# The last 16 keys of the scores in one padded block, and half of head 0's v transfers from ScalarE

## The chip, the cores and the metric

The kernel runs on one core of a Trainium2 chip. The metric is the device time of one execution, in microseconds (us).

## The reference

A two-layer encoder works on 272 tokens (16 learned meta tokens and 256 of the sequence) of width 1024. The change touches its first sub-layer alone, retention with four heads:

```python
q = rotary(q.astype(jnp.float32).reshape(B, T, RET_HEADS, RET_QK_DIM), pos)
k = rotary(k.astype(jnp.float32).reshape(B, T, RET_HEADS, RET_QK_DIM), pos) * (RET_QK_DIM ** -0.5)
...
s = jnp.einsum("bhid,bhjd->bhij", qc, kc) * intra_decay
o = jnp.einsum("bhij,bhje->bhie", s, vc) + jnp.einsum("bhid,bhde->bhie", qc, R) * q_decay
```

Taken in both directions this is, for each head, scores of all pairs of the 272 tokens, multiplied by gamma to the power of the tokens' distance, and then the product with v (512 columns for each head). Group norm, a gate and an output projection follow; then a gated convolutional MLP, a gated linear recurrence and a second MLP.

## The kernel before

All matrices are multiplied in two float16 parts. A float32 operand is split into a high part (its float16) and a low part (what is left), and each product is made of three: high with high, high with low, low with high (`three`, L1656 to L1660). The weights come from memory in chunks of 2 MB, each in two halves, into two `stage` buffers; ScalarE makes the high part (L548, the call `prep`) and VectorE the low part (L1008, also `prep`), in quarters. Four quarters make a chunk, and TensorE waits for each. TensorE's order is written out by hand, and so is every other engine's: each engine's program is one list in which an instruction that waits holds all that stand behind it.

For each head h the chunks are 3h (v's weights), 3h + 1 (q and k) and 3h + 2 (the gate). TensorE's order in a head is: values (chunk 3h, made at the end of the head before), q and k, gate, scores (L1908 to L1914), the values of the next head, for which it first waits on `g_out`, and the output products (L1922 to L1933). Behind them it waits for `v_out` of the next head before it takes chunk 3h + 4 (L1896).

- VectorE turns v out of PSUM by 32 x 32 blocks (`v_evict`, L1169 and L1170, raising `v_out`), rotates q and k (L1268 to L1271), makes their low parts (`qk_low`, L1241), evicts the gate (L1162, raising `g_out`), multiplies the scores by the decay (L1295), makes v's means (L1280) and low parts (L1285), and the low parts of the scores (L1303, L1304).
- ScalarE makes q's and k's high parts (`qk_high`, L700), scales v's rows (L719), makes v's high part (L726, L727) and that of the scores (L734 to L738), and does the gate's nonlinearity (L740).
- SyncE moves v from the 32 x 32 blocks into rows, in 16 transfers of 32 KB and 4 smaller ones for the last 16 tokens (`load_v_rows`, L472 to L482), each of which raises `v_landed`. In between it issues the chunk loads (L456).

The 272 tokens are cut into tiles of 128, 128 and 16 keys. The scores of a tile are a matmul with the keys as the stationary operand, for two halves k of the head's 256 features:

```python
for n, (m0, m) in enumerate(TOK_TILES):
    key = slice(m0, m0 + m)
    mm = three(ps[0:m, A + n, 0:T], qk_hi[:, 2 + k, key], qk_lo[:, 2 + k, key],
               qk_hi[:, k, :], qk_lo[:, k, :], k == 0, k == 1)
```

The output product of the last 16 keys is a single one already. Its 80 rows hold high scores at row 0, their low part at row 32 (`R_HI`) and the high scores again at row 64 (`R_LO`), against v's high, high and low parts (L1931).

Of the kernel before, what the change touches and what calls it, by code (L numbers as in the profile page):

```python
# [33 lines left out]
F16 = mybir.dt.float16  # L34
# [4 lines left out]
P = 128  # L39
# [109 lines left out]
def build(nc, tokens, gains, lru_pars, ffn_pars, chunks, ident, rope, decay, out):  # L149
    ctx = ExitStack()  # L150
    with ctx:
# [54 lines left out]
        rotq = carve(4, T)  # L206
        v_blocks = carve(4, 2 * P)
        v_edge = carve(4, 32)
        v_rows = carve(8, P)
# [19 lines left out]

        R_HI, R_LO = 32, 64  # L230

# [213 lines left out]
        def _(sp):  # L445
# [26 lines left out]
            def load_v_rows(h):  # L472

                sp.wait_ge(v_out, h + 1)
                from_blocks = v_blocks.rearrange("p e (n m) -> p (e n) m", m=P)
                for f in range(4):
                    for r in range(4):
                        rows, cols = slice(32 * r, 32 * (r + 1)), slice(32 * f, 32 * (f + 1))
                        sp.dma_start(v_rows[rows, :, cols], from_blocks[cols, :, rows]).then_inc(v_landed, 16)
# [47 lines left out]
        def _(act):  # L527
# [167 lines left out]
            for h in range(HEADS):  # L695
                c = RET_IN[h]

                def qk_high(x):
                    act.wait_ge(rot_done, 2 * h + x + 1)
                    act.activation(halves(qk_hi, x), halves(rotq, x), ACTF.Copy).then_inc(qkhi_made, 1)  # L700

                for q in range(3):
                    prep(c + 2, q)
                if h:
                    head_squares(h - 1)
                prep(c + 2, 3)
                for q in range(SUB if h else 1):
                    prep(c + 3, q)
# [12 lines left out]
                for n, (_, m) in enumerate(TOK_TILES):  # L721
                    act.wait_ge(vmean, NTT * h + n + 1)
                    if (h, n) == (0, 2):
                        act.wait_ge(zeroed, 1)
                    if n == 2:
                        act.activation(v_hi4[R_HI:R_HI + m, n], vs[n][0:m], ACTF.Identity, bias=vsum[0:m, n, 1:2])  # L726
                    act.activation(v_hi4[0:m, n], vs[n][0:m], ACTF.Identity,  # L727
# [7 lines left out]
                if h == 0:  # L735
                    act.wait_ge(zeroed, 2)
                act.activation(s_hi[R_LO:R_LO + META, 2, :], sT[0:META, 2, :], ACTF.Copy)
# [246 lines left out]
        def _(dve):  # L984
# [250 lines left out]
            for h in range(HEADS):  # L1235
# [3 lines left out]
                def qk_low(x):  # L1239
                    dve.wait_ge(qkhi_made, 2 * h + x + 1)  # L1240
                    dve.tensor_tensor(halves(qk_lo, x), halves(rotq, x), halves(qk_hi, x),  # L1241
                                      ALU.subtract).then_inc(qklo_made, 1)
# [51 lines left out]
                for n, (m0, m) in enumerate(TOK_TILES):  # L1294
                    last = dve.tensor_tensor(sT[0:m, n, :], ps[0:m, A + n, 0:T],  # L1295
                                             decay_sb[0:m, h, 2 * P - m0:2 * P - m0 + T], ALU.mult)
                last.then_inc(s_dec, 1)
                if h:
                    rsqrt(rs, A + 3, 0, ESTIMATE[("head", h - 1)])
                else:  # L1300
                    v_halves()
# [311 lines left out]
        def _(pool):  # L1613
# [25 lines left out]
            for n, size in enumerate((D, HEAD_V)):  # L1639
                pool.memset(ones_sb[:, n, :], 1.0 / size).then_inc(ones_set, 1)  # L1640
            pool.memset(v_hi[:, 2, :], 0.0).then_inc(zeroed, 1)
            pool.memset(s_hi[:, 2, :], 0.0).then_inc(zeroed, 1)
# [12 lines left out]
        def _(pe):  # L1655
# [236 lines left out]
            for h in range(HEADS):  # L1892
# [15 lines left out]
                for k in range(2):  # L1908
                    pe.wait_ge(qklo_made, 2 * h + k + 1)
                    for n, (m0, m) in enumerate(TOK_TILES):  # L1910
                        key = slice(m0, m0 + m)
                        mm = three(ps[0:m, A + n, 0:T], qk_hi[:, 2 + k, key], qk_lo[:, 2 + k, key],
                                   qk_hi[:, k, :], qk_lo[:, k, :], k == 0, k == 1)
                mm.then_inc(s_up, 1)  # L1914
# [9 lines left out]
                for e in range(4):  # L1924
# [3 lines left out]
                    for n in range(2):  # L1928
                        three(ps[:, A + e, 0:T], v_hi[:, n, col], v_lo[:, n, col], s_hi[:, n, :], s_lo[:, n, :],
                              n == 0, False)  # L1930
                    mm = pe.matmul(ps[:, A + e, 0:T], v_hi[0:R_LO + META, 2, col], s_hi[0:R_LO + META, 2, :],  # L1931
                                   start=False, stop=True)
# [280 lines left out]
```

## Time and profile before

| | |
|---|---|
| median of 3 runs | 708.3 us (708.06 to 708.33) |
| profiled execution | 708.33 us, span 706.5 us |
| TensorE busy | 695.9 us, 98% |
| VectorE busy | 610.5 us, 86% |
| ScalarE busy | 518.0 us, 73% |
| DMA | 134.31 MB, mean 190 GB/s |

The span runs from the first to the last recorded instruction; the time of the execution has 1.8 us more around it. Busy time of TensorE (PE) is modelled: a matmul of 272 columns is shown as 0.28 us long while the next one starts 0.12 us after it, so the starts are to be read, not the lengths. "Idle before" is the time in which an engine stood still ahead of a row, with what ended it.

### The profile page before, as it was taken

To read this page: it belongs to the slowest core of one execution; us is meant where nothing else is said; L and a number is where in the kernel's file an instruction comes from. 1 tells how busy PE (TensorE), PEld (TensorE's weight loads), DVE (VectorE), ACT (ScalarE), POOL (GpSimd) and SP (SyncE) were. 2 spreads that over 40 slices of the span, in tenths; PEclk is the share of its full clock that TensorE was granted. 3 is DMA by queue.
4 is the path that set the end of the run, shared out by engine and by line. 5 is a ranking of instruction groups with operands and counts; after the bars stand their busy time and mean duration, and the time that the engine had idled before them with its cause. 6 is when DMAs were issued, how large, how long until landed. Compare 5 with 4: busy or idle time off the path is not lost.

```text
span 706.5 us, 15923 instructions
## 1 busy us (share of the span) xinstructions
PE 695.9 (98%) x6495; PEld 584.7 (83%) x6495; DVE 610.5 (86%) x828; ACT 518.0 (73%) x834; POOL 25.7 (4%) x26
## 2 busy tenths in 40 slices
PE   8999999999999999999999999999999999999996
PEld 6888787887899888888889998888788888885464
DVE  6979897978789799989898879999999999999543
ACT  7477766757566888878787777999769888987431
POOL 0002020110100000000003000000000000000000
PEclk9999999999999999999999999999999999999999
DMA  9965646453481355655589951110625565566821
GB/s 348 309 250 149 240 140 250 131 175 147 180 321 48 133 217 188 229 178 178 187 307 397 350 192 61 62 60 1 234 92 211 195 223 208 208 237 207 260 41 60
DMA packets 47323, 134.31 MB, mean 190 GB/s; under 512 B 29728, under 2 KB 30240, under 8 KB 32032
## 3 DMA queue, kind: packets, MB, share of 16 engines
q1 hardware_dynamic: 46976, 133.20, 53.6%
q8 instruction: 39, 0.64, 0.4%
q10 hardware_dynamic: 288, 0.31, 0.1%
q14 instruction: 20, 0.16, 0.1%
HBM read 129.17 MB, written 1.05 MB: 184 GB/s over the span
## 4 chain that ended last, share of the span: by engine, by line
PE 89%; ACT 4%; DVE 4%; issue 1%; DMA 1%; SPq 0%; DVEq 0%; ACTq 0%
PE ps L1658 23%; PE ps L1660 22%; PE ps L1659 22%; PE ps L2094 3%; PE ps L2096 3%; PE ps L2095 3%; PE ps L1700 2%; PE ps L1705 2%; PE ps L1701 2%; PE ps L1782 1%; PE ps L1778 1%; PE ps L1779 1%; PE ps L2034 1%; DMA stage<-in_chunks 1%; ACT work L846 1%
## 5 line engine op out<-in xcount | busy, mean ns | idle before, releaser
L1658 PE MATMUL ps<-a_hi,w_hi 128*128 128x272 f16 (+1 forms) x1000 | 276.9, 277 | 0.3 <-DVE work L1170 0.3
L1660 PE MATMUL ps<-a_hi,w_lo 128*128 128x272 f16 (+1 forms) x1000 | 276.9, 277 | 0.0
L1659 PE MATMUL ps<-a_lo,w_hi 128*128 128x272 f16 (+1 forms) x1000 | 276.9, 277 | 0.0
L1008 DVE SCALAR_TENSOR_TENSOR w_lo<-stage,w_hi 128x1024 f16<-128x1024 f32 x207 | 247.8, 1227 | 26.4 <-ACT w_hi L548 26.1
L548 ACT ACTIVATE w_hi<-stage 128x1024 f16<-128x1024 f32 x207 | 210.1, 1047 | 50.6 <-PE ps L1660 21.6
L1658 PEld LDWEIGHTS ps<-a_hi,w_hi 128*128 128x128 f16 x1000 | 97.8, 98 | 17.1 <-issue 0.7
L1660 PEld LDWEIGHTS ps<-a_hi,w_lo 128*128 128x128 f16 x1000 | 97.8, 98 | 15.9
L1659 PEld LDWEIGHTS ps<-a_lo,w_hi 128*128 128x128 f16 x1000 | 97.9, 98 | 15.9
L1658 PE MATMUL ps<-y_hi,w_hi 128*128 128x272 f16 (+3 forms) x496 | 106.1, 242 | 0.0
L1659 PE MATMUL ps<-y_lo,w_hi 128*128 128x272 f16 (+3 forms) x496 | 106.1, 242 | 0.0
L1660 PE MATMUL ps<-y_hi,w_lo 128*128 128x272 f16 (+3 forms) x496 | 106.0, 242 | 0.0
L778 ACT ACTIVATE work<-work,cpar 128x272 f32<-128x272 f32 (+1 forms) x96 | 50.5, 596 | 40.4 <-DVE work L1162 40.4
L1658 PEld LDWEIGHTS ps<-y_hi,w_hi 128*128 128x128 f16 x496 | 48.5, 98 | 3.4 <-issue 0.2
L1659 PEld LDWEIGHTS ps<-y_lo,w_hi 128*128 128x128 f16 x496 | 48.5, 98 | 3.3
L1660 PEld LDWEIGHTS ps<-y_hi,w_lo 128*128 128x128 f16 x496 | 48.5, 98 | 3.0
L1359 DVE SCALAR_TENSOR_TENSOR work<-work,cpar 128x271 f32<-128x271 f32 (+1 forms) x96 | 40.9, 489 | 2.2 <-ACT work L778 2.2
L782 ACT ACTIVATE work<-work,cpar 128x271 f32<-128x271 f32 (+1 forms) x96 | 41.2, 500 | 0.0
L2096 PE MATMUL ps<-w_hi,y_lo 128*128 128x512 f16 (+1 forms) x120 | 40.4, 336 | 0.0
L2094 PE MATMUL ps<-w_hi,y_hi 128*128 128x512 f16 (+1 forms) x120 | 40.4, 336 | 0.0
L2095 PE MATMUL ps<-w_lo,y_hi 128*128 128x512 f16 (+1 forms) x120 | 40.4, 336 | 0.0
L1162 DVE TENSOR_TENSOR work<-ps,rs_in 128x1032 f32<-128x1032 f32 (+1 forms) x26 | 32.7, 1256 | 8.3 <-PE ps L1660 8.2
L1658 PE MATMUL ps<-work 128*128 128x272 f16 (+2 forms) x120 | 33.4, 278 | 0.5 <-ACT y_hi L836 0.5
(281 smaller groups left out, 1084.3 us busy)
## 6 DMA issues: line engine op xcount, KB each, us to landing
stage<-in_chunks SPq DMA_DIRECT2D x118, 1024.0 KB
work<-work SPq DMA_DIRECT2D x96, 32.0 KB, 2.0
stage<-in_chunks SPq DMA_DIRECT2D x3, 512.0 KB
decay_all<-in_decay SPq DMA_DIRECT2D x1, 1056.0 KB, 13.4
out<-sq SPq DMA_DIRECT2D x4, 256.0 KB, 2.0
hT<-in_tokens SPq DMA_DIRECT2D x3, 272.0 KB, 6.4
stage<-in_chunks SPq DMA_DIRECT2D x2, 256.0 KB
mT<-in_gains SPq DMA_DIRECT2D x1, 512.0 KB, 6.0
```

Of the source, the lines that this page charges most:

```text
L548: act.activation(part(0, c, q), flat(stage, c, q), ACTF.Copy, scale=W_SCALE).then_inc(whi_made, 1)
L778: last = act.activation(u_cv[b][:, n, t0:T], u_in[b][:, n, t0:T], ACTF.Identity, scale=tap_col(layer, j, 1, n), bias=tap_col(layer, j, 3, n))
L782: last = act.activation(u_left[:, n, t0:T - 1], u_in[b][:, n, t0:T - 1], ACTF.Copy, scale=tap_col(layer, j, 0, n))
L1008: dve.scalar_tensor_tensor(out=part(1, c, q), in0=flat(stage, c, q), scalar=W_SCALE, in1=part(0, c, q), op0=ALU.mult, op1=ALU.subtract).th ...
L1162: return dve.tensor_tensor(dst[:, :, t0:T], ps[:, first:first + 4, t0:T], rs_in[:, t0:T].unsqueeze(1).to_broadcast([P, 4, T - t0]), ALU.mult)
L1359: last = dve.scalar_tensor_tensor(out=u_cv[b][:, n, t0:T - 1], in0=u_in[b][:, n, t0 + 1:T], scalar=tap_col(layer, j, 2, n), in1=u_cv[b][:, ...
L1658: pe.matmul(o, w_h, x_h, start=start, stop=False)
L1659: pe.matmul(o, w_h, x_l, start=False, stop=False)
L1660: return pe.matmul(o, w_l, x_h, start=False, stop=stop)
L2094: pe.matmul(o, yh, wh[:, cols], start=k == 0, stop=False)
L2095: pe.matmul(o, yh, wl[:, cols], start=False, stop=False)
L2096: mm = pe.matmul(o, yl, wh[:, cols], start=False, stop=k == FT - 1)
```

## The change

It has two parts.

*Scores.* The stationary operand of the last 16 keys is no longer taken from `qk_hi` and `qk_lo`. A new tile `key_edge` of 2 x 128 columns, cleared once by GpSimd, gets the 16 keys' high part in columns 0 to 15 (ScalarE, in `qk_high`) and their low part in columns 32 to 47 (VectorE, in `qk_low`). Two products for each half k, with q's high and q's low part, take the place of three. Their rows 0 to 15 are then high keys by q, and rows 32 to 47 low keys by q. VectorE multiplies the second group by the decay on its own, right behind the rest, into row 96 (`R_KEY`) of the last scores tile, ScalarE copies v's high part to row 96 once more, and the output product takes 112 rows in place of 80.

*Transfers.* Of head 0's 16 transfers of v blocks, SyncE issues the first 8 and ScalarE the other 8, behind its fourth piece of the gate's weights. The other heads keep all 16 on SyncE.

```diff
+        key_edge = carve(P).bitcast(F16).rearrange("p (k c) -> p k c", k=2)
...
-                for f in range(4):
+                for f in range(4 if h else 2):
                     for r in range(4):
...
                     act.wait_ge(rot_done, 2 * h + x + 1)
+                    if (h, x) == (0, 0):
+                        act.wait_ge(zeroed, 1)
+                    act.activation(key_edge[:, x, 0:META], rotq[:, 2 + x, 2 * P:T], ACTF.Copy)
                     act.activation(halves(qk_hi, x), halves(rotq, x), ACTF.Copy).then_inc(qkhi_made, 1)
...
                 prep(c + 2, 3)
+                if h == 0:
+                    act.wait_ge(v_out, 1)
+                    for f in (2, 3):
+                        for r in range(4):
+                            rows, cols = slice(32 * r, 32 * (r + 1)), slice(32 * f, 32 * (f + 1))
+                            act.dma_start(v_rows[rows, :, cols], from_blocks[cols, :, rows]).then_inc(v_landed, 16)
...
                     if n == 2:
-                        act.activation(v_hi4[R_HI:R_HI + m, n], vs[n][0:m], ACTF.Identity, bias=vsum[0:m, n, 1:2])
+                        for row in (R_HI, R_KEY):
+                            act.activation(v_hi4[row:row + m, n], vs[n][0:m], ACTF.Identity, bias=vsum[0:m, n, 1:2])
...
                     dve.wait_ge(qkhi_made, 2 * h + x + 1)
+                    dve.tensor_tensor(key_edge[:, x, R_HI:R_HI + META], rotq[:, 2 + x, 2 * P:T], key_edge[:, x, 0:META],
+                                      ALU.subtract)
...
                 last.then_inc(s_dec, 1)
+                if h == 0:
+                    dve.wait_ge(zeroed, 3)
+                dve.tensor_tensor(s_hi[R_KEY:R_KEY + META, 2, :], ps[R_HI:R_HI + META, A + 2, 0:T],
+                                  decay_sb[R_HI:R_HI + META, h, R_HI:R_HI + T], ALU.mult)
...
+            pool.memset(key_edge[:], 0.0).then_inc(zeroed, 1)
...
-                    for n, (m0, m) in enumerate(TOK_TILES):
+                    for n, (m0, m) in enumerate(TOK_TILES[0:2]):
                         key = slice(m0, m0 + m)
-                        mm = three(ps[0:m, A + n, 0:T], qk_hi[:, 2 + k, key], qk_lo[:, 2 + k, key],
-                                   qk_hi[:, k, :], qk_lo[:, k, :], k == 0, k == 1)
+                        three(ps[0:m, A + n, 0:T], qk_hi[:, 2 + k, key], qk_lo[:, 2 + k, key],
+                              qk_hi[:, k, :], qk_lo[:, k, :], k == 0, k == 1)
+                    pe.matmul(ps[:, A + 2, 0:T], key_edge[:, k, :], qk_hi[:, k, :],
+                              start=k == 0, stop=False)
+                    mm = pe.matmul(ps[:, A + 2, 0:T], key_edge[:, k, :], qk_lo[:, k, :],
+                                   start=False, stop=k == 1)
...
-                    mm = pe.matmul(ps[:, A + e, 0:T], v_hi[0:R_LO + META, 2, col], s_hi[0:R_LO + META, 2, :],
+                    mm = pe.matmul(ps[:, A + e, 0:T], v_hi[0:R_KEY + META, 2, col], s_hi[0:R_KEY + META, 2, :],
                                    start=False, stop=True)
```

What each engine does where the change moves it, first ScalarE in head 0, from the last two pieces of the gate's weights (chunk 2) to those of head 1's values (chunk 3), before the change (a name behind "waits" is a semaphore):

```order
L548 ACTIVATE w_hi<-stage 128x1024 [waits w_used,w_landed0_1] x2
L548 ACTIVATE w_hi<-stage 128x1024 [waits w_used,w_landed1_0]
L700 ACTIVATE work<-work 128x2x272 [waits rot_done] x2
```

And the same place after it:

```order
L549 ACTIVATE w_hi<-stage 128x1024 [waits w_used,w_landed0_1] x2
L716 DMA work<-work 32x8x32 [waits v_out]
L716 DMA work<-work 32x8x32 x7
L549 ACTIVATE w_hi<-stage 128x1024 [waits w_used,w_landed1_0]
L703 ACTIVATE work<-work 128x16 [waits zeroed,rot_done]
L704 ACTIVATE work<-work 128x2x272
L703 ACTIVATE work<-work 128x16 [waits rot_done]
L704 ACTIVATE work<-work 128x2x272
```

Eight DMA issues stand ahead of the first piece of chunk 3, and a small copy ahead of each large one. Second, VectorE in head 0, from the low parts of q and k to v's means, before:

```order
L1241 TENSOR_TENSOR work<-work 128x2x272 [waits qkhi_made] x2
L1008 SCALAR_TENSOR_TENSOR w_lo<-stage,w_hi 128x1024 [waits w_used,whi_made] x3
L1162 TENSOR_TENSOR mT<-ps,rs_in 128x1088 [waits w_used]
L1295 TENSOR_TENSOR work<-ps,decay_all 128x272 [waits s_up]
L1295 TENSOR_TENSOR work<-ps,decay_all 128x272
L1295 TENSOR_TENSOR work<-ps,decay_all 16x272
L1280 TENSOR_SCALAR vsum<-vsum 128x1 [waits vs_out] x2
```

And after:

```order
L1252 TENSOR_TENSOR work<-work 128x16 [waits qkhi_made]
L1254 TENSOR_TENSOR work<-work 128x2x272
L1252 TENSOR_TENSOR work<-work 128x16 [waits qkhi_made]
L1254 TENSOR_TENSOR work<-work 128x2x272
L1019 SCALAR_TENSOR_TENSOR w_lo<-stage,w_hi 128x1024 [waits w_used,whi_made] x3
L1173 TENSOR_TENSOR mT<-ps,rs_in 128x1088 [waits w_used]
L1308 TENSOR_TENSOR work<-ps,decay_all 128x272 [waits s_up]
L1308 TENSOR_TENSOR work<-ps,decay_all 128x272
L1308 TENSOR_TENSOR work<-ps,decay_all 16x272
L1313 TENSOR_TENSOR work<-ps,decay_all 16x272 [waits zeroed]
L1293 TENSOR_SCALAR vsum<-vsum 128x1 [waits vs_out] x2
```

Two small subtractions stand among the low parts, and one more product with the decay ahead of the means.

## Rows read from the trace of the kernel before

**Rows 1.** The page's busy times, and the list of waits (us, times, longest).
```profile
PE 695.9 (98%) x6495; PEld 584.7 (83%) x6495; DVE 610.5 (86%) x828; ACT 518.0 (73%) x834; POOL 25.7 (4%) x26
...
PE ps L1658 <- DVE work L1170: 0.3, 1, 0.3
```

**Rows 2.** Timeline of TensorE, head 0 (start, us, what, idle before and its releaser).
```profile
43.79 0.29 PE L1658 MATMUL ps<-a_hi,w_hi 128*128 128x272 f16 x1
...
58.06 0.28 PE L1931 MATMUL ps<-work 80*128 80x272 f16 x1
58.61 0.29 PE L1658 MATMUL ps<-a_hi,w_hi 128*128 128x272 f16 x1 [0.27 <-DVE work L1170]
```

**Rows 3.** Timeline of ScalarE, head 0.
```profile
26.56 2.00 ACT L548 ACTIVATE w_hi<-stage 128x1024 f16<-128x1024 f32 x2 [0.49 <-DMA stage<-in_chunks]
29.05 1.06 ACT L548 ACTIVATE w_hi<-stage 128x1024 f16<-128x1024 f32 x1 [0.48 <-DMA stage<-in_chunks]
...
41.80 0.72 ACT L719 ACTIVATE work<-work,rs_tok 128x512 f32<-128x512 f32 x1 [1.80 <-DMA work<-work]
...
45.11 1.33 ACT L727 ACTIVATE work<-work,vsum 128x512 f16<-128x512 f32 x2 [1.09 <-DVE vsum L1280]
46.47 0.72 ACT L726 ACTIVATE work<-work,vsum 16x512 f16<-16x512 f32 x1
...
52.63 2.94 ACT L548 ACTIVATE w_hi<-stage 128x1024 f16<-128x1024 f32 x3
55.47 0.20 ACT L751 ACTIVATE lam<-par 128x16 f32<-128x16 f32 x1
```

**Rows 4.** Timeline of VectorE, head 0.
```profile
27.82 4.61 DVE L1008 SCALAR_TENSOR_TENSOR w_lo<-stage,w_hi 128x1024 f16<-128x1024 f32 x4
...
41.55 1.28 DVE L1162 TENSOR_TENSOR mT<-ps,rs_in 128x1088 f32<-128x1088 f32 x1
43.90 1.12 DVE L1295 TENSOR_TENSOR work<-ps,decay_all 128x272 f32<-128x272 f32 x3 [1.06 <-PE ps L1660]
...
53.70 3.50 DVE L1008 SCALAR_TENSOR_TENSOR w_lo<-stage,w_hi 128x1024 f16<-128x1024 f32 x3 [0.19 <-ACT w_hi L548]
...
58.28 0.27 DVE L1170 STREAM_TRANSPOSE work<-ps 128x128 f32<-128x128 f32 x1
```

**Rows 5.** Timeline of TensorE, scores of head 1.
```profile
81.32 0.28 PE L1658 MATMUL ps<-work 128*128 128x272 f16 x1
...
81.67 0.28 PE L1658 MATMUL ps<-work 128*128 128x272 f16 x1
...
81.90 0.28 PE L1660 MATMUL ps<-work 128*128 128x272 f16 x1
82.11 0.28 PE L1658 MATMUL ps<-work 128*16 128x272 f16 x1
...
83.59 0.28 PE L1660 MATMUL ps<-work 128*16 128x272 f16 x1
83.80 0.29 PE L1658 MATMUL ps<-a_hi,w_hi 128*128 128x272 f16 x1
```

**Rows 6.** DMA issues: SyncE's of v's rows (ns, then timeline), ScalarE's only two.
```profile
L479 SPq DMA_DIRECT2D work<-work x64: 591/611/1806, 25.5 to 146.8; - x64
...
25.46 11.79 SPq L479 DMA_DIRECT2D work<-work  x16
...
L673 ACTq DMA_DIRECT2D hT<-in_tokens x2: 404/428/452, 0.7 to 1.2; - x2
```

**Rows 7.** ScalarE's sequencer at L547 between 28 and 29 us.
```profile
L547 ACTq EVENT_SEMAPHORE  x1: 17/17/17, 28.3 to 28.3; - x1
```

**Rows 8.** Timeline of VectorE, heads 1 and 2.
```profile
81.41 1.29 DVE L1162 TENSOR_TENSOR mT<-ps,rs_in 128x1088 f32<-128x1088 f32 x1
...
120.64 1.29 DVE L1162 TENSOR_TENSOR mT<-ps,rs_in 128x1088 f32<-128x1088 f32 x1 [0.69 <-PE ps L1660]
123.48 1.12 DVE L1295 TENSOR_TENSOR work<-ps,decay_all 128x272 f32<-128x272 f32 x3 [1.55 <-PE ps L1660]
```

More of the change, by code:

```diff
@@ L207, in build @@
         v_blocks = carve(4, 2 * P)
+        from_blocks = v_blocks.rearrange("p e (n m) -> p (e n) m", m=P)
         v_edge = carve(4, 32)
@@ L228, in halves @@
             return v.rearrange("p (g x) t -> p x g t", x=2)[:, x]
-        R_HI, R_LO = 32, 64
+        R_HI, R_LO, R_KEY = 32, 64, 96
+        key_edge = carve(P).bitcast(F16).rearrange("p (k c) -> p k c", k=2)
         off = 0
@@ L474, in load_v_rows @@
                 sp.wait_ge(v_out, h + 1)
-                from_blocks = v_blocks.rearrange("p e (n m) -> p (e n) m", m=P)
-                for f in range(4):
+                for f in range(4 if h else 2):
                     for r in range(4):
@@ L723, in _ @@
                     if (h, n) == (0, 2):
-                        act.wait_ge(zeroed, 1)
+                        act.wait_ge(zeroed, 2)
                     if n == 2:
-                        act.activation(v_hi4[R_HI:R_HI + m, n], vs[n][0:m], ACTF.Identity, bias=vsum[0:m, n, 1:2])
+                        for row in (R_HI, R_KEY):
+                            act.activation(v_hi4[row:row + m, n], vs[n][0:m], ACTF.Identity, bias=vsum[0:m, n, 1:2])
                     act.activation(v_hi4[0:m, n], vs[n][0:m], ACTF.Identity,
@@ L735, in _ @@
                 if h == 0:
-                    act.wait_ge(zeroed, 2)
+                    act.wait_ge(zeroed, 3)
                 act.activation(s_hi[R_LO:R_LO + META, 2, :], sT[0:META, 2, :], ACTF.Copy)
```

## The prediction

> **What bounds the kernel now.** I began with the busy times and the list of waits: TensorE is busy for 98% of the span, and in the four heads it waits for another engine's result once after the start, 0.3 us for VectorE's transpose at L1170 [rows 1]. So a change in the heads is worth what it takes from TensorE's row of matmuls, less every new wait. The second view is TensorE's timeline around the scores; the third is ScalarE's and VectorE's timelines in head 0, where the reader is to see that both are busy almost without a gap from 43.9 us until VectorE hands head 1 its banks.
>
> The one wait is larger than 0.3 us: the last output product of head 0 starts at 58.06, the next matmul could start at 58.18 and starts at 58.61, so 0.43 us are lost; the transpose at 58.28 ends at 58.55 [rows 2, 4]. The chain behind it begins with the end of the scores, for which VectorE's multiplication by the decay waits until 43.90; the mean behind that lets ScalarE start the halves of v at 45.11 after 1.09 us of idle; ScalarE runs on to the weight piece that begins at 52.63 and ends at 53.7, and VectorE needs three pieces and the transpose from there [rows 3, 4]. In head 0 TensorE and this chain end 0.43 us apart, and the chain is the longer.
>
> **TensorE.** Two products in a row start 0.115 us apart. Head 1's scores run from 81.32 to 83.80, 2.48 us for 18 products, where 18 x 0.116 make 2.09. The missing 0.39 lies in four places: 81.90 to 82.11 before a block of 16 columns, 83.59 to 83.80 behind one, and the same twice more [rows 5]. No such gap stands between the two full blocks: the second starts at 81.67, three products behind 81.32. With the last block 128 columns wide and two products for its three, 16 x 0.116 = 1.86 us are left: **0.63 us less per head**, 0.23 from two products and about 0.39 from four gaps. The output product has 112 rows for 80 and the same 128 columns. I cost it at nothing; gaps like those above on both sides of each of its four would be 0.8 us per head, and nothing in the rows asks for them.
>
> **Small operations.** Per head ScalarE gets two copies of 128x16 and one more copy of v's last rows (16x512); VectorE gets two subtractions of 128x16 and one decay product of 16x272. A 128x16 operation takes 0.20 us on ScalarE [rows 3], and I take at most that on VectorE; the copy of v is 0.72 us [rows 3]; the decay product adds 1.12/3 = 0.36 us [rows 4]. GpSimd's extra clearing lies in the first microseconds, hidden behind the first loads.
>
> **The eight transfers on ScalarE.** An issue of this shape takes SyncE 0.61 us, and 16 of them 11.79 us with one of 1.8 us among them, or 0.66 us from start to start otherwise [rows 6]. ScalarE's only issues in the trace, of plain rows, take 0.43 us; SyncE's of v are nearest in shape, so I take 0.66; 0.45 and twice 0.66 are the ends that the rivals price. When do they begin? The two activations at 26.56 wait for a stage that lands at 26.5. ScalarE's sequencer passed the next wait at 28.3, when the second of them still ran until 28.56 [rows 3, 7]: it runs ahead of its engine. So the issues begin at about 26.7 and end at 26.7 + 8 x 0.66 = 32.0. Behind them stands the first piece of chunk 3 (29.05 now): it ends at about 33.1. VectorE wants its result as the fourth of the pieces that begin at 27.82, at 31.27 [rows 4]. **VectorE loses 1.8 us**, and from there to 42.83 it has no more than 0.2 us of idle to give back. What the move buys is no term: v's rows now land at 41.8 [rows 3], after a wait of 1.8 us, and still ScalarE's next step stands idle for 1.09 us, for the mean behind the scores. SyncE's loads go out 5 us earlier, for stages that nobody waits for there.
>
> **Head 0.** VectorE's multiplication at L1162, for which TensorE waits before head 1's values, ends at 42.83 [rows 4], now at 42.83 + 0.17 (key copies) + 1.8 = 44.8. TensorE, done with the scores at 43.79 - 0.63 = 43.16 [rows 2], waits 1.7 us there. VectorE takes up the decay at 44.75 instead of 43.90 (+0.85); the extra product makes the mean +1.2; ScalarE's extra copy of v, in a stretch with no idle, +0.72: the transpose comes 1.95 us later, and TensorE with it, its earlier wait being inside this sum. Head 0: **+1.95**. Without any delay by the issues the decay would begin 0.54 us earlier, with the last score product (of the 0.63 the last gap lies behind it), and the sum be -0.54 + 0.36 + 0.72 = **+0.54**: even then the head loses, since its gain lies on TensorE and its costs on the chain that ends last. VectorE would be free for the decay at 42.92 and take it up at 43.36, so the first 0.44 us of delay cost nothing.
>
> **Head 1.** L1162 stands behind v's last rows here. It runs from 81.41 to 82.70 while TensorE needs it at 83.80 [rows 5, 8], 83.17 after the change. The extra copy delays it by 0.72, the key copies and subtractions by 0.3: it ends at 83.72. TensorE waits 0.6 us and keeps next to nothing: **0.0**.
>
> **Heads 2 and 3.** L1162 waited for TensorE by 0.69 us, and the decay product by another 1.55 [rows 8]. Of the 1.02 us that delay it in head 1, 0.33 are left: it ends at 121.93 + 0.33 = 122.26. TensorE wants it 0.11 before the decay product starts, as in head 0 (43.79 and 43.90), at 123.37, now 122.74. The rest follows TensorE. **-0.63 each, -1.26.** Later stages touch nothing of the change.
>
> **Sum.** 1.95 + 0.0 - 1.26 = +0.7 us. The profiled execution took 708.33 us (span 706.5), 0.03 above the median of 708.3. Forecast: **709.0 us**. A measurement here tells 0.2%, 1.4 us, from no change: under 706.9 is faster, over 709.7 slower.
>
> One page speaks against my largest term. The trace has 0.61 us for an issue of v's rows, and I count it in full [rows 6]. The Trainium skill, "DMA: Bandwidth & Descriptors", section "Issuing engines are not separate DMA queues", calls the time that a sequencer takes to initiate a DMA "usually small relative to the DMA itself". With eight issues at nothing the sum is -0.7 and the time 707.6 us. No row here shows an issue so short.
>
> **The rivals.**
> (a) *The issues are cheap on ScalarE.* For it: 0.43 us for its two plain ones. Eight at 0.45 us from start to start end at 30.3, the piece at 31.4, and VectorE loses 0.2, under the free 0.44. Sum 0.54 + 0.0 - 1.26 = -0.7: **707.6 us**. The page named above, of the Trainium skill, comes out here too. Against it: the 64 issues of this shape on SyncE, none under 0.59. Chance 0.2.
> (b) *The issues are dear: slower.* They wait until ScalarE's engine has drained (28.56), or two queues that issue at once slow each other; one of SyncE's issues took 1.8 us [rows 6]. Beginning at 28.56 they end at 33.9, the piece at 35.0, VectorE loses 3.7, head 0 costs 3.85: sum +2.6, **710.9 us**. It decides from 2.5 us of delay on, that is, from a last issue that ends after 32.7, 0.75 us per issue. Two queues in turn at twice the time would give some +5.5. For the drained engine nothing speaks in the rows; against it stands the wait passed at 28.3 [rows 7]. Chance 0.22.
> (c) *The added work hides.* If the extra copy and product fall into gaps that I overlook, the heads 1 to 3 keep 0.63 each and head 0 stays: -1.9, **706.4 us**. Against it: no idle between 45.11 and 53.7 on ScalarE. Chance 0.12.
> (d) *The gaps stay.* They belong to the change of block, not to 16 columns: 0.23 per head. Head 0 and head 1 are held by VectorE anyway; heads 2 and 3 give 0.46: +1.5, **709.8 us**. Against it: no gap between the full blocks. Chance 0.06.
>
> **How the numbers follow.** The forecast has 0.4, and of it a little lies over 709.7, if one issue is long. Faster: (c) and some of (a), where head 1 keeps its part, 0.14. Slower: (b), (d) and that little, 0.28. Within 0.2%: 0.58. The range goes from 707.2, below (a), to 711.0, just over (b), and leaves out most of (c) and the double price.
>
> **What would show it.** The scores of each head take 1.86 us with even spacing. ScalarE's issues stand from 26.7 to 32.0 at about 0.6 us; the first piece of chunk 3 starts there at 32, and VectorE waits some 1.8 us for it. TensorE waits 1.7 us at the start of head 1's values, some 1.3 us for the transpose, 0.6 us in head 1, and nothing in heads 2 and 3. ScalarE no longer waits for v's rows. I am wrong if VectorE's wait is under 0.5 or over 2.5 us, if heads 2 and 3 are not 0.6 us shorter each, or if a wait appears behind the heads.

## The result, and the profile after

| | before | after |
|---|---|---|
| median of 6 runs | 708.16 us (708.05 to 708.33) | 711.6 us (711.08 to 711.97) |
| profiled execution | 708.33 us, span 706.5 us | 711.7 us, span 709.9 us |
| TensorE busy | 695.9 us | 696.4 us |
| VectorE busy | 610.5 us | 614.5 us |
| ScalarE busy | 518.0 us | 522.0 us |

The ratio is 1.0048 (95%: 1.0035 to 1.0061), 3.4 us more. The forecast was 709.0 us and the range ended at 711.0: the kernel is slower, and by more than the range held. Here a head runs on TensorE from its first product with q's and k's weights to the same of the next head. Head 0 is counted from its scores on, and head 3 to the product that follows its last output product. Read so from TensorE's timelines, the heads took (us):

| | head 0 | head 1 | head 2 | head 3 |
|---|---|---|---|---|
| before | 17.30 | 39.58 | 39.57 | 32.66 |
| after | 22.61 | 38.94 | 38.93 | 32.36 |
| difference | +5.31 | -0.64 | -0.64 | -0.30 |
| forecast | +1.95 | 0.0 | -0.63 | -0.63 |

The differences sum to +3.73; the scores of head 0 start 0.36 us earlier by the span's origin (40.95 for 41.31), and +3.37 is what the span shows. So the loss lies in head 0 alone. The waits of the heads in TensorE's list, us in total, times, longest:

```profile
PE ps L1676 <- DVE mT L1173: 3.4, 1, 3.4
...
PE ps L1676 <- DVE work L1321: 0.2, 1, 0.2
```

Before, the list had one wait in the heads, 0.3 us for the transpose [rows 1]. Now it has 3.4 us for the gate's eviction (L1173, which was L1162) in head 0, and none for the transpose; the 0.2 us at L1321 are head 3's, taken up further down. TensorE's timeline of head 0, from the last products of the scores on:

```profile
42.58 0.28 PE L1932 MATMUL ps<-work 128*128 128x272 f16 x1
42.69 0.28 PE L1934 MATMUL ps<-work 128*128 128x272 f16 x1
46.35 0.41 PE L1676 MATMUL ps<-a_hi,w_hi 128*128 128x272 f16 x1 [3.38 <-DVE mT L1173]
46.55 0.43 PE L1677 MATMUL ps<-a_lo,w_hi 128*128 128x272 f16 x1
46.77 0.43 PE L1678 MATMUL ps<-a_hi,w_lo 128*128 128x272 f16 x1
47.00 0.43 PE L1676 MATMUL ps<-a_hi,w_hi 128*128 128x272 f16 x1
```

Two things are to be seen. The first is the wait: the next product could have started at 42.81 and starts at 46.35. The second is the spacing behind it: 0.227 us from product to product where it was 0.116. The table by stretches (us; busy time and count of PE, PEld, DVE, ACT and POOL; granted clock; DMA share; GB/s) names the cause:

```profile
45.00:46.00 1.00, 0.00 (x0) 0.00 (x0) 1.00 (x2) 0.57 (x2) 0.00 (x0) 0.67 1.04 442
46.00:48.00 2.00, 1.65 (x8) 1.10 (x9) 1.96 (x8) 0.01 (x1) 0.00 (x0) 0.50 1.01 422
48.00:50.00 2.00, 2.00 (x11) 1.28 (x10) 1.32 (x4) 1.98 (x3) 0.00 (x0) 0.50 0.74 299
50.00:52.00 2.00, 2.00 (x11) 1.28 (x10) 0.59 (x2) 1.98 (x4) 0.00 (x0) 0.50 0.00 0
52.00:53.00 1.00, 1.00 (x9) 0.82 (x8) 0.32 (x1) 1.00 (x2) 0.00 (x0) 0.92 0.00 0
```

From 46 to 52 us the granted clock is 0.50, 1.2 GHz in place of 2.4. TensorE had stood still for 3.4 us before, and the clock had already fallen by the end of that wait (0.67 from 45 to 46 us). The 27 products from 46.35 on took 5.96 us where full clock gives 27 x 0.116 = 3.13.

Why the eviction came late stands on ScalarE, whose issues are the rows at ACTq, and on VectorE:

```profile
26.79 1.06 ACT L549 ACTIVATE w_hi<-stage 128x1024 f16<-128x1024 f32 x1 [0.48 <-DMA stage<-in_chunks]
26.89 1.69 ACTq L716 DMA_DIRECT2D work<-work  x2
27.76 1.04 ACT L549 ACTIVATE w_hi<-stage 128x1024 f16<-128x1024 f32 x1
28.60 4.75 ACTq L716 DMA_DIRECT2D work<-work  x6
33.45 1.06 ACT L549 ACTIVATE w_hi<-stage 128x1024 f16<-128x1024 f32 x1 [4.66 <-PE ps L1678]
```

```profile
27.46 3.47 DVE L1019 SCALAR_TENSOR_TENSOR w_lo<-stage,w_hi 128x1024 f16<-128x1024 f32 x3
34.54 1.23 DVE L1019 SCALAR_TENSOR_TENSOR w_lo<-stage,w_hi 128x1024 f16<-128x1024 f32 x1 [3.61 <-ACT w_hi L549]
...
45.01 1.28 DVE L1173 TENSOR_TENSOR mT<-ps,rs_in 128x1088 f32<-128x1088 f32 x1
46.21 1.11 DVE L1308 TENSOR_TENSOR work<-ps,decay_all 128x272 f32<-128x272 f32 x3
47.35 0.44 DVE L1313 TENSOR_TENSOR work<-ps,decay_all 16x272 f16<-16x272 f32 x1
47.81 0.26 DVE L1293 TENSOR_SCALAR vsum<-vsum 128x1 f32<-128x1 f32 x3
...
62.02 0.27 DVE L1181 STREAM_TRANSPOSE work<-ps 128x128 f32<-128x128 f32 x1
```

The issues run from 26.89 to 33.35, the first piece of chunk 3 begins at 33.45 (29.05 before [rows 3]), and VectorE, which had run through here in one row of four [rows 4], stands still for 3.61 us. Two issues were long (the durations are ns, least/median/greatest); the first row is ScalarE's, the second SyncE's:

```profile
L716 ACTq DMA_DIRECT2D work<-work x8: 633/646/1408, 26.9 to 32.7; - x8
```

```profile
L480 SPq DMA_DIRECT2D work<-work x56: 592/611/1908, 25.1 to 150.8; - x56
```

The 1.408 us issue of ScalarE runs from 30.61 to 32.02, SyncE's of 1.908 from 30.2 to 32.1. SyncE's 1.806 of before [rows 6] ran from 30.21 to 32.02. A long issue at the same time in three records is no accident, and I had read it as one. With the experiments there are fourteen traces, and each has it.

### The profile page after: what moved, and what is told of

Read it like the earlier page. It is cut to its first block, busy times and chain, and to the rows that moved or that the text cites. A ratio compares the mean times of both kernels' runs of the same rounds, so it can differ in the third digit from the quotient of the medians.

```text
span 709.9 us, 15933 instructions
## 1 busy us (share of the span) xinstructions
PE 696.4 (98%) x6487; PEld 586.8 (83%) x6487; DVE 614.5 (87%) x840; ACT 522.0 (74%) x846; POOL 24.1 (3%) x27
## 4 chain that ended last, share of the span: by engine, by line
PE 85%; DVE 5%; ACT 5%; DMA 2%; issue 1%; ACTq 1%; DVEq 0%
PE ps L1676 22%; PE ps L1677 22%; PE ps L1678 22%; PE ps L2117 3%; PE ps L2118 3%; PE ps L2116 3%; DMA stage<-in_chunks 2%; PE ps L1723 1%; PE ps L1719 1%; PE ps L1718 1%; PE ps L1800 1%; PE ps L1796 1%; PE ps L1797 1%; PE ps L2056 1%; ACTq L716 1%
## 5 line engine op out<-in xcount | busy, mean ns | idle before, releaser
L1173 DVE TENSOR_TENSOR work<-ps,rs_in 128x1032 f32<-128x1032 f32 (+1 forms) x26 | 32.6, 1256 | 8.3 <-PE ps L1678 8.2
L1676 PE MATMUL ps<-work 128*128 128x272 f16 (+1 forms) x112 | 31.1, 277 | 0.7 <-ACT y_hi L847 0.5
```

The source lines that it names most:

```text
L1173: return dve.tensor_tensor(dst[:, :, t0:T], ps[:, first:first + 4, t0:T], rs_in[:, t0:T].unsqueeze(1).to_broadcast([P, 4, T - t0]), ALU.mult)
L1676: pe.matmul(o, w_h, x_h, start=start, stop=False)
```

## The experiments

Each kernel ran beside the kernel before on the same chip. Line numbers in their rows are their own, so some differ by a few lines from those above.

**The two parts apart.** First the scores alone:

```diff
-                for f in range(4 if h else 2):
+                for f in range(4):
...
-                if h == 0:
-                    act.wait_ge(v_out, 1)
-                    for f in (2, 3):
...
```

> The changed kernel with all 16 v transfers back on SyncE: the padded scores block alone. Theory 1 (the loss is the eight issues ahead of chunk 3's first weight piece, with the clock's fall behind them): VectorE's idle of 3.6 us ahead of that piece is gone, TensorE does not wait ahead of head 1's values, head 0 costs 0.5 us against the kernel before (the chain to the transpose), head 1 gives 0.0 and heads 2 and 3 give 0.64 each: about 0.7 us faster than before, 707.5 us. Rival (the padded block or the added small operations cost what was lost): 711 us or more.

Measured: 707.76 us, ratio 0.9996 (0.9987 to 1.0005). Heads 18.20, 39.44, 38.93, 32.36: +0.90, -0.14, -0.64, -0.30. So the change of the scores alone is worth nothing that can be measured, and the forecast's shape holds: head 0 loses, head 1 keeps next to nothing, and TensorE now waits for VectorE. From its list of waits the transpose of head 0 and, from its timeline, head 1's values:

```profile
PE ps L1670 <- DVE work L1175: 1.8, 1, 1.8
```

```profile
83.86 0.28 PE L1928 MATMUL ps<-work 128*128 128x272 f16 x1
84.46 0.29 PE L1670 MATMUL ps<-a_hi,w_hi 128*128 128x272 f16 x1 [0.32 <-DVE mT L1167]
```

Second, the moved transfers alone, with the scores as before:

```diff
-                for f in range(4):
+                for f in range(4 if h else 2):
...
                 prep(c + 2, 3)
+                if h == 0:
+                    act.wait_ge(v_out, 1)
+                    for f in (2, 3):
+                        for r in range(4):
...
```

> The kernel before with eight of head 0's v transfers issued by ScalarE, nothing else changed. Theory 1: the eight issues take 5.3 to 6.5 us, VectorE waits some 3.5 us for chunk 3's first piece and TensorE some 2.4 us for the gate's eviction. If TensorE's clock falls after that wait as it does in the changed kernel, some 25 products run at half speed, +2.8 us, and head 0 costs +4.8: 713.0 us. If it stays up, the transpose comes 2.1 us later: 710.3 us. Rival (the issues hurt only together with the scores' part): within 0.5 us of before.

Measured: 712.31 us, ratio 1.0054 (1.004 to 1.0068). Head 0 took 21.62 us, +4.32, and the others were as before. The moved transfers are the whole loss. VectorE's wait is that of the full change (3.87 us for 3.61), and TensorE waits for the same eviction:

```profile
35.00 1.23 DVE L1014 SCALAR_TENSOR_TENSOR w_lo<-stage,w_hi 128x1024 f16<-128x1024 f32 x1 [3.87 <-ACT w_hi L548]
```

```profile
PE ps L1664 <- DVE mT L1168: 3.0, 1, 3.0
```

**The issues where nobody waits.** ScalarE issues its eight behind the first piece of chunk 3:

```diff
                 prep(c + 2, 3)
+                for q in range(SUB if h else 1):
+                    prep(c + 3, q)
                 if h == 0:
                     act.wait_ge(v_out, 1)
...
-                for q in range(SUB if h else 1):
-                    prep(c + 3, q)
```

> The changed kernel with ScalarE's eight issues one step later, behind chunk 3's first piece, where ScalarE stood idle for 4.4 us. Theory 1 (only their place ahead of that piece costs): VectorE has no wait of over 0.5 us there, and the time is that of the scores' part alone, 707.5 us. Rival (issues from two queues disturb each other or the transfers themselves cost): SyncE's issues lengthen and the time stays over 709 us.

Measured: 708.0 us, ratio 0.9998 (0.9988 to 1.0007); head 0 took 18.20 us, what it took without the move. The eight issues are about as long as in the change (6.76 us for 6.46), and only a small copy stands behind them:

```profile
29.26 6.76 ACTq L718 DMA_DIRECT2D work<-work  x8
36.13 0.22 ACT L703 ACTIVATE work<-work 128x16 f16<-128x16 f32 x1 [5.82 <-issue]
```

The held issue is here too (ScalarE's third, 2.03 us from 30.68). It is the place of the issues ahead of the piece that costs, and not a slower landing of v's rows or the load on the queues.

**Half as many.** Four issues in place of eight, at the place of the change:

```diff
-                for f in range(4 if h else 2):
+                for f in range(4 if h else 3):
...
-                    for f in (2, 3):
+                    for f in (3,):
```

> The changed kernel with ScalarE issuing four of head 0's v transfers in place of eight. Theory 1 (what counts is when the last issue ends): four issues from 26.9 end at 29.7, before the stretch from 30.1 to 32.1 in which an issue of either queue stood still in every trace so far; the first piece of chunk 3 ends at about 30.9, when VectorE wants it, and the time is that of the scores' part alone, 707.8 us. Rival (issues on ScalarE cost as such): half of the loss, 709.7 us.

Measured: 707.96 us, ratio 0.9998 (0.9989 to 1.0007), head 0 again 18.20. The four end before the time at which issues are held, and VectorE has no gap:

```profile
28.46 1.51 ACTq L716 DMA_DIRECT2D work<-work  x2
30.08 1.06 ACT L549 ACTIVATE w_hi<-stage 128x1024 f16<-128x1024 f32 x1 [1.38 <-PE ps L1678]
```

```profile
27.65 4.74 DVE L1019 SCALAR_TENSOR_TENSOR w_lo<-stage,w_hi 128x1024 f16<-128x1024 f32 x4
```

So the loss is not in proportion to the number of issues: half of them cost nothing, all of them the whole. The run does not say how much of the loss is the held issue's, since four issues from 26.8 on end in time for VectorE whether a hold follows or not.

**The clock.** Does the half clock cost the 2.8 us that the spacing shows? Here TensorE multiplies 28 times into a bank that nobody reads while it would wait, before head 1's values; the dummy products are the only difference from the change:

```diff
                 mm.then_inc(s_up, 1)
 
+                if h == 0:
+                    for _ in range(28):
+                        pe.matmul(ps[:, A + 3, 0:T], a_hi[:, 0, 0:P], a_hi[:, 1, :], start=True, stop=True)
                 pe.wait_ge(g_out, h + 1)
```

> The changed kernel with 28 matmuls of no use (about 3.25 us) in head 0 between the scores and the wait for the gate's eviction. Theory 2 (the clock fell because TensorE stood idle for 3.4 us): the granted clock stays at 2.4 GHz, head 1's values start 0.116 us apart at once, 2.8 us are saved on TensorE, of which the chain to the transpose and head 1's wait leave about 0.6: 711.0 us, while the transpose becomes the wait of head 0 (TensorE waits some 1.2 us for it). Rival (the fall has another cause, such as the padded block or the small operations): the same half clock from 46 us on, 711.6 us or more.

Measured: 711.79 us, ratio 1.0052 (1.0038 to 1.0065), against 711.6 for the change, where 711.0 was expected. The granted clock stays at 1.00, so in the change it was TensorE's standing still that let it fall, and the wait returns behind the values, for the transpose:

```profile
48.00:50.00 2.00, 2.00 (x20) 1.69 (x18) 1.31 (x6) 1.62 (x3) 0.00 (x0) 1.00 0.90 377
```

```profile
PE ps L1676 <- DVE work L1181: 1.4, 1, 1.4
```

Head 0 is 0.98 us shorter than in the change (21.63), head 1 0.50 longer (39.44, as in the scores alone): with a slow TensorE, VectorE had its transposes ready 1.3 us early (62.29 for 63.56) and came ahead in head 1. By these heads the clock costs 0.5 us in net. But the issues were longer in this trace (VectorE's wait 3.85 us for 3.61), which hides 0.24 us; with them an estimate of the net cost is 0.7 us. The times show none of it, and their executions lie 0.7 to 0.9 us apart. The 2.8 us lay mostly where TensorE would have waited anyway.

**The gaps.** The kernel before, with the last block of keys read 128 columns wide (m0 = T - 128), and then 64 wide. Both leave the scores of the last 16 keys out: the rows that are read belong to other keys.

```diff
                     for n, (m0, m) in enumerate(TOK_TILES):
+                        if n == 2:
+                            m0, m = T - 128, 128
                         key = slice(m0, m0 + m)
```

> The kernel before, with the last tile's stationary block made of the last 128 keys in place of the last 16: three products still, 18 per head. (Of its 128 rows the following steps take the first 16 as before, which belong to other keys; the scores of the last 16 keys are thus not computed.) Theory A (the gaps of 0.1 us belong to the narrow block): no gap, 2.09 us for the scores in place of 2.48, 0.39 us less in heads 1, 2 and 3, and nothing in head 0, which the transpose holds: 706.9 us. Rival B (the gaps belong to the change of tile or output rows): the four gaps stay, 708.1 us.

> As e5, with the last 64 keys as the block. (The scores of the last 16 keys are not computed here either.) If anything under the full 128 columns brings the gap, the gaps are those of 16 columns, 0.1 us each: 708.1 us. If they follow the width, they are between: about 707.5 us.

Measured: 128 wide 706.69 us, ratio 0.9981 (0.9972 to 0.999), 18 products in 2.08 us; 64 wide 708.28, ratio 1.0002 (0.9993 to 1.0012), 2.52 us. Two pieces of TensorE's timeline in head 1, 128 wide and then 64 wide:

```profile
81.81 0.28 PE L1660 MATMUL ps<-work 128*128 128x272 f16 x1
81.93 0.28 PE L1658 MATMUL ps<-work 128*128 128x272 f16 x1
```

```profile
81.89 0.28 PE L1660 MATMUL ps<-work 128*128 128x272 f16 x1
82.09 0.30 PE L1658 MATMUL ps<-work 128*64 128x272 f16 x1
...
82.35 0.28 PE L1660 MATMUL ps<-work 128*64 128x272 f16 x1
82.56 0.29 PE L1658 MATMUL ps<-work 128*128 128x272 f16 x1
```

The gap comes with a block narrower than 128 columns, 64 or 16 alike, on the way in and out; width is what removes it. Four gaps are worth 0.4 us per head, and the two spared products the other 0.23. Removed without new work on the other engines, the gaps alone give 1.4 us.

**The work on the chain.** The scores alone, with ScalarE's extra copy of v behind the next weight piece, where it had stood ahead of the main copy:

```diff
-                        for row in (R_HI, R_KEY):
-                            act.activation(v_hi4[row:row + m, n], vs[n][0:m], ACTF.Identity, bias=vsum[0:m, n, 1:2])
+                        act.activation(v_hi4[R_HI:R_HI + m, n], vs[n][0:m], ACTF.Identity, bias=vsum[0:m, n, 1:2])
...
+                act.activation(v_hi4[R_KEY:R_KEY + META, 2], vs[2][0:META], ACTF.Identity, bias=vsum[0:META, 2, 1:2])
```

> The scores' part alone with v's third copy (0.72 us) behind the next weight piece instead of ahead of the main copy. In head 0 it stays on the chain to the transpose: +0.9 us as before. In head 1 the gate's eviction comes 0.7 us earlier, TensorE does not wait, and head 1 gives 0.64 in place of 0.14: 0.5 us faster than the scores' part alone, 707.3 us. If head 1 stays at 0.14, its wait has another cause.

Measured: 707.78 us, ratio 1.0002 (0.9993 to 1.0011). In the trace head 1 took 38.94 us, the full -0.64, and head 0 18.33. The times don't show the 0.5 us that was expected (707.3): they fell into two groups, seven of 707.36 to 707.85 and four of 709.0 to 709.4, and this run decides nothing by its median. The four had a mean granted clock of 0.996, the seven 0.998 or 0.999, so the clock may have fallen behind head 0's wait in them too; none of the four was traced, and that is not shown. That the copy is what held head 1 rests on the trace.

Then the kernel before with nothing changed but the order in head 0: both engines take chunk 4's pieces ahead of the gate's nonlinearity and of the parameters' scaling.

```diff
+                if h == 0:
+                    for q in range(1, SUB):
+                        prep(c + 4, q)
                 act.wait_ge(g_out, h + 1)
                 act.activation(gT, gT, ACTF.Silu, scale=-0.5 * UNSCALE).then_inc(g_silu, 1)
```

> The kernel before with only the new order in head 0 (chunk 4's first piece earlier on VectorE, the gate's nonlinearity behind the other three on ScalarE). The transpose ends before TensorE wants it, so the 0.43 us lost in head 0 come back and nothing else: 707.7 us. If it gave more, part of e8's gain would be the order's and not the padded block's.

Measured: 707.79 us, ratio 0.9995 (0.9986 to 1.0004); head 0 took 16.87, 0.43 less, and its wait for the transpose is gone. The size is what the trace of before let one read [rows 2]; alone it is under what the times tell.

Both together, with the extra decay product behind the low parts of the scores and two semaphores of their own for the late rows:

```diff
+                if h == 0:
+                    prep(c + 4, 1)
+                    prep(c + 4, 2)
+                    key_copy()
+                    prep(c + 4, 3)
...
+                dve.tensor_tensor(s_hi[R_KEY:R_KEY + META, 2, :], ps[R_HI:R_HI + META, A + 2, 0:T],
+                                  decay_sb[R_HI:R_HI + META, h, R_HI:R_HI + T], ALU.mult).then_inc(skey_made, 1)
```

> The scores' part alone, with the work that it adds taken off the chains: v's third copy behind the next weight piece (in head 0 behind three), the extra decay product behind the scores' low parts, both with signals of their own that only the 112-row product waits for; in head 0 VectorE makes the first piece of chunk 4 while it waits for ScalarE, and ScalarE makes the other three before the gate's nonlinearity. Theory (what the scores' part lost, it lost on the chain to the transpose in head 0, 0.9 us, by the wait for the gate's eviction in head 1, 0.5, and by that for the scores' low parts in head 3, 0.34): TensorE waits nowhere in the heads; 4 times 0.64 and the 0.43 us that head 0 lost before are gained: 3.0 us, 705.1 us. Rival (the gain of the products is not to be had): 707.5 us or more.

Measured: 706.71 us, ratio 0.998 (0.9971 to 0.9989), where 705.1 was expected. Heads 16.23, 39.87, 38.93, 32.12. Head 0 gave 1.07; head 1 lost 0.3, since TensorE waits 0.8 us for its gate. VectorE had stood idle for chunk 5's pieces, because ScalarE's nonlinearity and the loads of its tables now stood ahead of them:

```profile
58.22 3.50 DVE L1026 SCALAR_TENSOR_TENSOR w_lo<-stage,w_hi 128x1024 f16<-128x1024 f32 x3 [1.32 <-ACT w_hi L551]
```

Another 0.5 us is lost behind the heads. The heads and their earlier start make 2.3 us less at the end of head 3, and the span is only 1.7 less: in the output projection TensorE waits for VectorE's step at L1197, which it did not do before. The next kernel has the same wait, and this is its row:

```profile
171.98 0.70 PE L1902 MATMUL ps<-sq,ones_sb 128*128 128x272 f32 x2 [0.24 <-DVE mT L1197]
```

It starts 0.4 us later than it could. VectorE's row from the decay products of head 3 to L1197 takes 10.51 us in that trace and 9.98 in the kernel before, and the late second decay product stands in it with 0.47. That it is the cause is read from these rows; no run moved it alone.

For head 1, the work on the recurrence's parameters was moved one head later:

```diff
-                if h == 0:
+                if h == 1:
                     act.wait_ge(par_raw, 1)
...
-                if h == 1:
+                if h == 2:
                     lru_series()
...
-                if h == 2:
+                if h == 3:
                     lru_rates()
```

> The run with the added work off the chain lost 0.8 us in head 1, where TensorE waited for the gate's eviction; VectorE had stood idle for 1.32 us at 58.2 for chunk 5's pieces, behind 1.7 us of ScalarE's parameter work (an activation of 0.20, a table load of 1.28, one of 0.22). Here that parameter work is moved to the end of head 1, and the two groups of VectorE's parameter work one head later each (the first, 2.9 us, from head 1 to head 2). Theory (that idle is the cause): no wait at the gate in head 1, head 1 38.9 to 39.1 us in place of 39.87, the others as there (16.2, 38.9, 32.1); 705.9 us where the other run had 706.7. Rival (the 2.9 us on VectorE only move the wait to head 2, and ScalarE's 1.7 us with them): head 1 38.9, head 2 39.5 or more, 706.5 us or over.

Measured: 706.0 us, ratio 0.9971 (0.9961 to 0.9982). Heads 16.23, 38.93, 39.22, 32.13: head 1's wait is gone, and 0.27 us of it came back in head 2, half of what the rival theory had. There the gate's eviction ends at 120.84, and TensorE, free at 120.62, goes on at 120.89 (VectorE's timeline, then TensorE's):

```profile
119.55 1.29 DVE L1180 TENSOR_TENSOR mT<-ps,rs_in 128x1088 f32<-128x1088 f32 x1
```

```profile
120.50 0.28 PE L1940 MATMUL ps<-work 128*128 128x272 f16 x1
120.89 0.29 PE L1682 MATMUL ps<-a_hi,w_hi 128*128 128x272 f16 x1
```

**The gaps without the work.** Last, the order-only kernel with a wide view of the keys: the last block reads on into the slot behind it, so its first 16 columns are the right keys and the rest gives rows that nobody reads. q's and k's low parts moved to a place of their own; no operation is added on ScalarE or VectorE.

```diff
+                if h == 0:
+                    pe.wait_ge(zeroed, 2)
+                for k in range(2):
+                    mm = three(ps[:, A + 2, 0:T], wide_hi[k], wide_lo[k],
+                               qk_hi[:, k, :], qk_lo[:, k, :], k == 0, k == 1)
```

> This is the kernel before with the order of the order-only run (head 0's pieces of chunk 4 ahead of the gate's nonlinearity) and a wide view: the last block is 128 columns long and taken straight from the buffers of q's and k's parts, so that its first 16 columns are the right keys and its other rows of the result are not read; three products as before, both halves k at the end of the scores; no operation is added on ScalarE or VectorE. Gap theory (a gap of 0.1 us into and out of each narrow block): the scores take 2.08 us in each head. No work is added on the chain, so every head keeps its 0.39 us: head 0 is 0.43 (order) + 0.29 to 0.39 shorter than the kernel before's 17.3 us, that is 16.5; heads 1 and 2 39.19, head 3 32.3. Sum -1.9 us: 706.2 us beside 708.1. Rival (the order's 0.43 us and the gaps hide each other in head 0): head 0 16.9, sum -1.5, 706.6 us.

Measured: 706.21 us, ratio 0.9973 (0.9964 to 0.9983), where 706.2 was expected. Heads 16.46, 39.17, 39.16, 32.36; scores 2.08. It has three products where the change has two, but no copy, no subtraction and no second decay product. The 0.5 us behind the heads are not lost here. The two last kernels can't be told apart by their times, 706.0 and 706.21, and both beat the kernel before by 2 us and the change by more than 5. The wide view is much the smaller edit.

## Why the prediction was wrong

By its own steps:

- **The scores, -0.63 per head: right.** They take 1.85 us with even spacing, and the 64-column run confirms that the width is what counts. Rivals (c) and (d) fall with it: the added work did not hide in head 0 (+0.90 for the scores alone), and the gaps did not stay.
- **The eight transfers: the step that failed.** "So the issues begin at about 26.7 and end at 26.7 + 8 x 0.66 = 32.0" and "VectorE loses 1.8 us". They began at 26.89 and ended at 33.35, and VectorE stood still for 3.61. A common issue took 0.65 us, as I had taken. What I missed is that issues are held at a fixed place in the program: between 30.1 and 32.1 us one issue of each queue that issues is long, in the kernel before too, where the row had said 1806 ns [rows 6]. I took the 1.8 us out of the mean as a stray. But the hold is less than half of the 1.8 us by which VectorE's wait exceeds the forecast. ScalarE's held issue took 1.41 us for 0.64, which is 0.77. The first two took 0.74 and 0.92, 0.38 more than common ones; the row began 0.19 later than forecast; the piece's own steps took 0.1 more; and VectorE was free at 30.93 and not at 31.27, 0.34 earlier. By this count VectorE would have waited 2.8 us with no hold at all (an estimate), so the price of a common issue was right and the sum around it too small. The table of stretches from 30 to 32 us, for before and then after:

```profile
30.00:32.00 2.00, 2.00 (x20) 1.69 (x18) 2.00 (x3) 0.11 (x1) 0.00 (x0) 1.00 1.20 98
```

```profile
30.00:32.00 2.00, 2.00 (x19) 1.69 (x18) 0.93 (x1) 0.00 (x0) 0.00 (x0) 1.00 1.56 137
```

  The DMA share there is over 1, while only 98 and 137 GB/s move; from 26 to 28 us it was 430. The engines were busy with small packets: from 30 to 32 us 1151 of the 1157 packets of the kernel before are under 512 bytes. That this holds the issues is argued from the coincidence; no run changed it alone. A count of issues is a second reading: SyncE's held issue is the eighth of its row in all fourteen traces, so for SyncE number and time can't be told apart. ScalarE's was the sixth in three traces and the third where its issues began at 29.26, so there it goes by the time. The outcome was rival (b)'s, with its deciding point: a last issue that ends after 32.7. It came at 33.35. Its reasons were not: the issues did not wait for the engine to drain (they began at 26.89), and SyncE's were held in the kernel before, where no second queue issued. It had named SyncE's long issue only as a sign. The Trainium skill, "DMA: Bandwidth & Descriptors", section "Issuing engines are not separate DMA queues", calls this time usually small relative to the DMA itself. The trace agrees for a single one, 0.65 us beside 4.3 from issue to landing. But eight in a row held ScalarE's queue for 6.5 us, and could not be counted as nothing, nor at rival (a)'s 0.45 us each.
- **Head 0, +1.95: +5.31.** With the clock held up it is +4.33, in a trace where VectorE waited 3.85 us: 2.05 more than forecast for the issues, and 0.36 in the small work (the scores alone cost +0.90 where I had +0.54; the second decay product puts the first mean 0.55 us later and not 0.36, and the rest lies in smaller shifts). In the change itself the issues are 1.8 over the forecast, and the clock's fall adds about 1.2 in head 0, which nothing in the forecast held.
- **Head 1, 0.0: -0.64 in the change, but by luck.** At full clock it is -0.14, in the scores alone and in the busy-wait run alike, with the wait for the gate that I forecast (0.32 to 0.5 us for 0.6). In the change it vanished because the slow stretch had let VectorE get ahead.
- **Heads 2 and 3, -0.63 each: -0.64 and -0.30.** In head 3 I overlooked a wait. Head 3 has no values of a next head to cover VectorE, only 36 products, and its output products wait for the scores' low parts, which stand behind the second decay product:

```profile
170.54 0.28 PE L1676 MATMUL ps<-work 128*128 128x272 f16 x1 [0.22 <-DVE work L1321]
```

- **Behind the heads: as forecast.** After head 3 the trace is 3.4 us later than that of before, as the whole span is. ScalarE no longer waits for v's rows, and it gained nothing by it: it waited 2.43 us for v's mean in their place, at 47.99.

From +0.7 to +3.4 the sum goes thus: in head 0 the issues +1.8, the small work +0.36 and the clock +1.2, the clock -0.50 in head 1, head 1 otherwise -0.14, head 3 +0.33, head 2 -0.01, the earlier start of head 0 -0.36; together +2.7.

## What to carry to other kernels

Look up where in time the longest instruction of a group stands before you call it a stray, and ask whether what you move will pass that place. And let a forecast of a delay start from the slack that is there: here VectorE came 0.34 us earlier than in the trace of before, and that was a fifth of the error in its wait. A DMA issue on a computing engine costs its queue's time for all that stands behind it, so put issues behind the work that others wait for: the same eight were free one instruction later. And when the bound engine is given less to do, see first that the engine which feeds it is not given more: the same gaps closed by a wider view, with no new work, were worth 2 us with a better order.

## What was not expected of the hardware

- An issue of SyncE stood still until about 32 us (31.6 to 32.9) in all fourteen traces, always its row's eighth, begun at 29.8 to 30.4: for 1.3 to 2.8 us, 1.8 to 2.0 in the kernel before, the change and the runs with moved transfers. Where ScalarE issued at that time one of its issues was held too, for 1.4 to 2.0 us, its sixth or its third. Four issues that ended at 29.97 escaped it.
- After 3.4 us in which TensorE waited, the granted clock was 0.50 (1.2 GHz) until 52.2, some 6 us of work. In the run with the moves alone TensorE waited 3.0 us, went on at 46.70 at full clock, and the clock fell one microsecond later, to 0.50 for 3.4 us:

```profile
46.00:48.00 2.00, 1.30 (x11) 1.05 (x12) 1.85 (x7) 0.23 (x1) 0.00 (x0) 0.93 1.02 422
48.00:50.00 2.00, 2.00 (x10) 1.32 (x9) 1.42 (x2) 1.96 (x4) 0.00 (x0) 0.50 0.89 352
```

  In the traces with waits of 1.9 us and less it stayed at 1.00 in the heads. Products then started 0.227 us apart in place of 0.116. In the change it cost 2.8 us of matmul time and some 0.7 us of the kernel's, by the estimate above.
- A matmul whose stationary block has 64 columns pays the same 0.1 us on the way in and on the way out as one with 16; with 128 there is no gap. A block of 112 rows and 128 columns (the output product) has none either.
- ScalarE's sequencer issues a DMA while its engine still computes: the first two issues stand at 26.89, ahead of an activation that began at 27.76 and comes before them in the program.
